# Attention transposes taken from TensorE to VectorE and DMA, in two sets of query blocks

## The chip, the cores and the metric

The kernel runs on one core of one Trainium2 chip. The metric is the device time of one execution in microseconds (us), the median of several runs. The kernel before takes 1697.11 us (three runs, 1695.94 to 1697.37).

## The reference, cut to what matters

The program is two transformer blocks one after the other over 512 tokens of width 1024. The change touches only the attention of the first block. It has 8 heads of width 64. Keys lie in two blocks of 256; each query sees all earlier keys (with two blocks, the selection of past blocks takes the one there is), so what is computed is plain causal attention with a distance bias:

```
s = q @ k^T * 64**-0.5 - slope[head] * (query - key), masked where key > query
p = softmax(s)
out[query] = sum over keys of p[query, key] * v[key]
y_attn = out @ w_branch_attn
```

The last product contracts over keys. TensorE contracts over partitions, so for it both v and p must lie with the key on the partition. The projection leaves v with the head's columns on the partitions, and the softmax runs with the query on the partitions. Both must be turned.

## The kernel before

**Matrix products in three parts.** Every float32 product is made of three: weights are split into a rounded part w_hi (ScalarE, L1259, 128x2048) and the rest w_lo (GpSimd, L454, four pieces of 128x512), the operand into a_hi and a_lo. A tile of 128 output columns by 512 tokens takes 24 matmuls of 128x512: 16 against w_hi (L504 and L505) and 8 against w_lo (L511). Weights come in panels of 1 MB, two tiles each, into two buffers w_raw, loaded by SyncE (L418) as soon as w_lo of the panel two before is made.

**A pair of heads.** `pair_of_heads` on TensorE runs four times, the first in straight code, the other three as a loop. One pair has four panels and eight tiles: q, k, v, a pool input, and four gate tiles. In order: tiles 0 to 3, between whose thirds stand the score products of the four query blocks (`scores`, L655); `turn_v`, four transposes of 128x128 (L661) of v_s into the PSUM bank aux 2; tile 4 (in the first pair it stands ahead of `turn_v`); tiles 5, 6 and 7, behind whose nine thirds `turn_probs` (L672) is spread, eight calls with 4, 4, 3, 3, 2, 2, 1 and 1 transposes; then `values` (L681), eight matmuls of probs_t with v_n. So TensorE makes 24 transposes in each pair, 96 in all.

**The other engines in a pair.** VectorE (L1855 to L1874) takes each score block from PSUM, adds the distance bias, finds the row's maximum, and one step later divides the exponentials (ScalarE, L1305) by their sum; then it stores tiles 4 to 7. Block qt of a head lies in `probs[head][:, qt, :]` and has 128 (qt + 1) keys. ScalarE copies each turned bank into v_n (L1319) and probs_t (L1312), with the rounding of the weights of panel 4i+4 between the fourth and the fifth of these, and that of 4i+5 after the last. Then it copies the pair's result (L1326), and VectorE makes its low part (L1881).

**What sets the order.** Each engine runs its instructions in written order and waits on semaphores. SyncE's queue before holds nothing in this stage but the loads of the weights. An instruction that waits holds up all behind it on its engine.

## Time and profile before

| | |
|---|---|
| median of three runs | 1697.11 us |
| span of the profiled execution, first to last instruction | 1694.9 us |
| TensorE busy | 1684.5 us (99%) |
| VectorE, ScalarE, GpSimd busy | 874.7, 706.1, 793.1 us (52%, 42%, 47%) |
| DMA moved | 193.84 MB, mean 114 GB/s |
| granted TensorE clock, mean | 0.997 |
| the four pairs of heads | 0 to 221 us |

The page's last matmul ends some microseconds before the span does, and of what a run's time holds around the span the profile shows nothing; the median lies 2.2 us above the span. To read the table: TensorE is busy nearly without a gap. How busy the other engines are says little by itself; what counts is when their results come.

### The profile page before, as it was taken

The numbers are of one execution on the slowest core, as the hardware profiler recorded it, in microseconds if no ns is written. First come the engines' busy times: TensorE is split into PE (matmuls) and PEld (weight loads), VectorE is DVE, ScalarE is ACT, GpSimd is POOL, SyncE is SP. The second block draws the span as 40 slices with busy tenths as digits, with TensorE's granted clock in tenths as the row PEclk, the third lists the DMA queues.
The fourth block names the chain that finished last, engine by engine and source line by source line (L and its number), as shares of the span: only waits on it lengthen the run. The fifth ranks groups of instructions, "written<-read, shape, count | busy, mean of one in ns | idle before, by whom it ended". The sixth has DMA issues, their size and how long they took to land.

```text
span 1694.9 us, 21874 instructions
## 1 busy us (share of the span) xinstructions
PE 1684.5 (99%) x7963; PEld 1374.6 (81%) x7963; DVE 874.7 (52%) x1365; ACT 706.1 (42%) x977; POOL 793.1 (47%) x605
## 2 busy tenths in 40 slices
PE   9999999999999999999999999999999999999998
PEld 7777778788888888888878888788888888888887
DVE  6234374563616167797897878863355511101113
ACT  5333364431313134456464554784424422222232
POOL 2434354444545455543434344444545544654453
PEclk9999999999999999999999999999999999999999
DMA  5222222274636342233222332222222222332232
GB/s 187 99 75 74 74 104 82 81 261 157 229 117 225 122 151 100 93 106 125 100 100 101 117 104 99 99 75 99 76 99 100 76 98 99 129 127 91 99 124 100
DMA packets 32540, 193.84 MB, mean 114 GB/s; under 512 B 3648, under 2 KB 5696, under 8 KB 13792
## 3 DMA queue, kind: packets, MB, share of 16 engines
q1 hardware_dynamic: 25376, 158.89, 26.5%
q10 hardware_dynamic: 7104, 34.15, 5.8%
q8 instruction: 38, 0.62, 0.1%
q14 instruction: 22, 0.18, 0.0%
HBM read 190.86 MB, written 2.16 MB: 114 GB/s over the span
## 4 chain that ended last, share of the span: by engine, by line
PE 98%; DMA 0%; DVE 0%; ACT 0%; SPq 0%; issue 0%; DVEq 0%
PE gemm_bank L511 25%; PE gemm_bank L504 25%; PE gemm_bank L505 25%; PE gemm_bank L542 4%; PE gemm_bank L558 4%; PE gemm_bank L551 3%; PE gemm_bank L546 1%; PE gemm_bank L789 1%; PE aux_bank L975 1%; PE aux_bank L655 1%; PE aux_bank L980 1%; PE aux_bank L960 1%; PE aux_bank L681 1%; PE aux_bank L672 1%; DMA w_raw<-weights_dram 0%; PE aux_bank L953 0%
## 5 line engine op out<-in xcount | busy, mean ns | idle before, releaser
L454 POOL TENSOR_TENSOR w_lo<-w_raw,w_hi 128x512 fp32r<-128x512 f32 x580 | 771.5, 1362 | 881.6 <-ACT w_hi L1259 870.4
L504 PE MATMUL gemm_bank<-a_hi,w_hi 128*128 128x512 f32 x1008 | 402.6, 399 | 0.0
L505 PE MATMUL gemm_bank<-a_lo,w_hi 128*128 128x512 f32 x1008 | 393.2, 390 | 0.0
L1259 ACT ACTIVATE w_hi<-w_raw 128x2048 fp32r<-128x2048 f32 x145 | 276.5, 1907 | 187.1 <-PE gemm_bank L511 122.7
L504 PE MATMUL gemm_bank<-b_hi,w_hi 128*128 128x512 f32 x688 | 267.8, 389 | 0.0
L505 PE MATMUL gemm_bank<-b_lo,w_hi 128*128 128x512 f32 x688 | 267.7, 389 | 0.0
L511 PE MATMUL gemm_bank<-a_hi,w_lo 128*128 128x512 f32 x1024 | 258.7, 395 | 0.0
L511 PEld LDWEIGHTS gemm_bank<-a_hi,w_lo 128*128 128x128 f32 x1024 | 190.2, 188 | 45.0 <-issue 6.2
L504 PEld LDWEIGHTS gemm_bank<-a_hi,w_hi 128*128 128x128 f32 x1008 | 189.3, 188 | 43.9 <-issue 5.6
L505 PEld LDWEIGHTS gemm_bank<-a_lo,w_hi 128*128 128x128 f32 x1008 | 189.4, 188 | 39.4 <-issue 1.9
L2161 DVE SCALAR_TENSOR_TENSOR aux_bank<-scratch,gcol,aux_bank 128x511 f32<-128x511 f32 (+15 forms) x240 | 165.8, 734 | 14.2 <-ACT aux_bank L1485 11.9
L511 PE MATMUL gemm_bank<-b_hi,w_lo 128*128 128x512 f32 x688 | 170.6, 389 | 0.0
L511 PEld LDWEIGHTS gemm_bank<-b_hi,w_lo 128*128 128x128 f32 x688 | 129.1, 188 | 26.8
L505 PEld LDWEIGHTS gemm_bank<-b_lo,w_hi 128*128 128x128 f32 x688 | 129.2, 188 | 26.8
L504 PEld LDWEIGHTS gemm_bank<-b_hi,w_hi 128*128 128x128 f32 x688 | 129.1, 188 | 26.7
L2461 DVE TENSOR_TENSOR arena<-arena,gemm_bank 128x512 f32<-128x512 f32 x21 | 14.4, 688 | 174.6 <-PE gemm_bank L511 173.1
L2394 DVE SCALAR_TENSOR_TENSOR h<-gemm_bank,mod,h 128x512 f32<-128x512 f32 x23 | 17.3, 751 | 108.6 <-PE gemm_bank L511 104.9
L504 PE MATMUL gemm_bank<-f_hi,w_hi 128*128 128x512 f32 x165 | 64.2, 389 | 0.0
L505 PE MATMUL gemm_bank<-f_lo,w_hi 128*128 128x512 f32 x165 | 64.2, 389 | 0.0
L1735 ACT ACTIVATE f_hi<-arena 128x512 f32 (+1 forms) x22 | 13.9, 632 | 115.9 <-DVE arena L2461 115.0
L2202 DVE SCALAR_TENSOR_TENSOR sq<-gemm_bank,gcol,sq 128x511 f32<-128x511 f32 (+2 forms) x72 | 53.8, 748 | 13.2 <-ACT sq L1505 11.5
L1393 ACT ACTIVATE b_hi<-gemm_bank 128x512 fp32r<-128x512 f32 x31 | 18.6, 599 | 100.5 <-DVE gemm_bank L2006 100.5
(414 smaller groups left out, 2133.4 us busy)
## 6 DMA issues: line engine op xcount, KB each, us to landing
w_raw<-weights_dram SPq DMA_DIRECT2D x146, 1024.0 KB, 4.7
arena<-ada_dram ACTq DMA_DIRECT2D x32, 768.0 KB, 4.7
acc<-cum_rows ACTq DMA_DIRECT2D x8, 512.0 KB, 3.7
h<-x_t_dram SPq DMA_DIRECT2D x8, 256.0 KB, 5.9
row_b<-cum_rows ACTq DMA_DIRECT2D x4, 512.0 KB, 4.8
scratch<-cum_rows ACTq DMA_DIRECT2D x4, 512.0 KB, 4.2
out_t_dram<-a_raw SPq DMA_DIRECT2D x7, 256.0 KB, 2.2
w_raw<-weights_dram SPq DMA_DIRECT2D x4, 256.0 KB, 5.2
```

Source lines behind the costliest of these rows:

```text
L454: ins = pool.tensor_tensor(wlo[s][:, w], raw[s][:, w], whi[s][:, w].bitcast(F32), ALU.subtract)
L504: pe.matmul(gemm_bank[bank][:, :], whi[slot][:, w], hi[:, k, :], start=(n == 0), stop=False)
L505: pe.matmul(gemm_bank[bank][:, :], whi[slot][:, w], lo[:, k, :], start=False, stop=False)
L511: mm = pe.matmul(gemm_bank[bank][:, :], wlo[slot][:, blk * P:blk * P + P], hi[:, k, :], start=False, stop=(n == last))
L542: pe.matmul(gemm_bank[t % 4][:, :], whi[panel % 2][:, w], hi[:, k, :], start=(n == 0), stop=False)
L551: pe.matmul(gemm_bank[t % 4][:, :], wlo[panel % 2][:, blk * P:blk * P + P], hi[:, k, :], start=False, stop=False)
L558: mm = pe.matmul(gemm_bank[t % 4][:, :], whi[panel % 2][:, blk * P:blk * P + P], lo[:, k, :], start=False, stop=(n == last))
L1259: act.activation(whi[panel % 2][:, :], raw[panel % 2][:, :], ACT.Copy).then_inc(w_hi_ready, 1)
L1393: act.activation(b_hi[:, j, :], bank, ACT.Square).then_inc(b_hi_ready, 1)
L2161: dve.scalar_tensor_tensor(aux[q][:, d:S], u_buf[:, q, 0:S - d], gc(G_CONV_W + CONV_TAPS * q + CONV_TAPS - 1 - d), aux[q][:, d:S], ALU.mul ...
L2202: ins = dve.scalar_tensor_tensor(acc[:, d:S], bank[:, 0:S - d], gc(G_SSM_W + SSM_TAPS * n + SSM_TAPS - 1 - d), acc[:, d:S], ALU.mult, ALU.add)
L2394: dve.scalar_tensor_tensor(hk, gemm_bank[t % 4][:, :], g_, hk, ALU.mult, ALU.add).then_inc(h_ready, 1)
```

## The change

v and the probabilities are no longer turned by TensorE.

- VectorE turns 32x32 blocks (`dve.transpose`): v_s into turned_v once v is stored and the pool tile is stored, and each query block of each head into `turned_p` as soon as it is divided by its sum. Within a partition it writes the blocks in another order, so that a transfer has rows of 128 elements.
- SyncE stores these to DRAM (`store_turned`, 256 KB each in pieces of 512 B: two for each query block, one for v) and loads them back with the 32-partition groups exchanged (four transfers for v, and in `move_turned` eight transfers of 128 KB for each half of the query blocks, each into 32 partitions). A load waits until the stores it needs have landed.
- ScalarE copies from the loaded squares into v_n and probs_t (`in_place`), query blocks 0 and 1 first, then the rounding of panel 4i+4, then blocks 2 and 3.
- TensorE's tiles 5 to 7 run without anything between; `values` waits for ScalarE's nine copies (values_ready).
- The loads of the weights now stand in SyncE's queue among these transfers: panels 4i+3 and 4i+4 ahead of them, 4i+5 and 4i+6 behind them.
- GpSimd clears the first three blocks of both turned_p at the start. Three semaphores are merged with others or dropped.

```
-                def turn_v():
-                    pe.wait_ge(bank_free[2], 2 * i + 2)
-                    for t in range(QT):
-                        mm = pe.transpose(aux[2][:, t * P:(t + 1) * P], v_s[:, t * P:(t + 1) * P], ident[:, :])
-                    mm.then_inc(t_done, 1)
-
-                def turn_probs(n):
...
-                    for qt in range(j, QT):
-                        mm = pe.transpose(bank[:, qt * P:(qt + 1) * P], probs[head][:, qt, j * P:(j + 1) * P], ident[:, :])
...
                 def values():
-                    pe.wait_ge(t_read, 9 * i + 9)
+                    pe.wait_ge(values_ready, 9 * i + 9)
...
+            def store_turned(i, qt, count):
+                sp.wait_ge(turned, 9 * i + count)
+                for head in range(2):
+                    sp.dma_start(probs_dram[head][:, :, qt, :], turned_p[head][:, qt, :].rearrange("k (g x) -> k g x", g=QT)) \
+                        .then_inc(turned_stored, 16)
+            def move_turned(first, end):
+                for head in range(2):
+                    to = turned_p[head][:, first:end, :].rearrange("k t n -> k (t n)").rearrange("k (p x) -> k p x", p=QT)
+                    rows = probs_dram[head].rearrange("(p k) g t x -> k p g t x", p=QT)[:, :, :, first:end, :] \
+                        .rearrange("k p g t x -> k p g (t x)")
+                    for g in range(QT):
+                        sp.dma_start(to[32 * g:32 * g + 32], rows[:, :, g, :]).then_inc(probs_moved, 16)
+            load(2, 0)
+            with sp.Fori(0, PAIRS) as i:
+                load(4 * i + 3, 1)
+                load(4 * i + 4, 0)
+                store_turned(i, 0, 2)
+                store_turned(i, 1, 4)
+                sp.wait_ge(turned, 9 * i + 5)
+                sp.dma_start(v_dram, turned_v.rearrange("k (g x) -> k g x", g=QT)).then_inc(turned_stored, 16)
+                sp.wait_ge(turned_stored, 16 * 9 * i + 16 * 5)
+                rows = v_dram.rearrange("(p k) g x -> k p g x", p=QT)
+                for g in range(QT):
+                    sp.dma_start(v_raw[32 * g:32 * g + 32, :].rearrange("k (p x) -> k p x", p=QT), rows[:, :, g, :]) \
+                        .then_inc(v_moved, 16)
+                move_turned(0, 2)
+                store_turned(i, 2, 7)
+                store_turned(i, 3, 9)
+                sp.wait_ge(turned_stored, 16 * 9 * i + 16 * 9)
+                move_turned(2, 4)
+                load(4 * i + 5, 1)
+                load(4 * i + 6, 0)
...
+                def in_place(half):
+                    act.wait_ge(probs_moved, 256 * i + 128 * half + 128)
...
+                        for t in range(2):
+                            qt = 2 * half + t
+                            act.activation(probs_t[head][:, 0:qt + 1, qt * P:(qt + 1) * P].rearrange("k j (p e) -> k j p e", p=QT),
+                                           moved[:, t, 0:qt + 1, :, :], ACT.Copy).then_inc(values_ready, 1)
...
+                        dve.wait_ge(bank_free[2], 2 * i + 2)
+                        dve.transpose(turned_v.rearrange("q (g c e) -> q c g e", g=QT, c=QT),
+                                      v_s.rearrange("q (c g e) -> q c g e", c=QT, g=QT)).then_inc(turned, 1)
...
+                            dve.wait_ge(probs_ready, 8 * i + u + 1)
+                            dve.transpose(turned_p[head][:, qt - 1, :].rearrange("k (g j e) -> k j g e", g=QT, j=QT)[:, 0:qt, :, :],
+                                          probs[head][:, qt - 1, 0:n].rearrange("q (j g e) -> q j g e", j=qt, g=QT)) \
+                                .then_inc(turned, 1)
```

On TensorE, at the end of the first pair of heads, the rows before are these (gemm_bank3 is tile 7, aux_bank0 and aux_bank2 take the turned probabilities, L681 is `values`):

```order
L505 MATMUL gemm_bank3<-a_lo_49,w_hi1 128x512
L504 MATMUL gemm_bank3<-a_hi,w_hi1 128x512
L505 MATMUL gemm_bank3<-a_lo_49,w_hi1 128x512
L672 MATMUL aux_bank0<-ident,arena 128x128 [waits t_read]
L672 MATMUL aux_bank2<-ident,scratch 128x128 [waits t_read]
L511 MATMUL gemm_bank3<-a_hi,w_lo1 128x512 x8
L681 MATMUL aux_bank3<-arena 64x512 [waits b_lo_ready,t_read]
L681 MATMUL aux_bank3<-scratch,arena 64x512
```

and in the changed kernel, at the same place:

```order
L550 MATMUL gemm_bank3<-a_lo_49,w_hi1 128x512
L549 MATMUL gemm_bank3<-a_hi,w_hi1 128x512
L550 MATMUL gemm_bank3<-a_lo_49,w_hi1 128x512
L556 MATMUL gemm_bank3<-a_hi,w_lo1 128x512 x8
L709 MATMUL aux_bank3<-arena,row_b 64x512 [waits b_lo_ready,values_ready]
L709 MATMUL aux_bank3<-scratch,row_b 64x512
```

The transposes between the thirds of a tile are gone, and the first matmul of `values` waits for ScalarE's copies instead of the last turned bank.

On SyncE, the whole loop that loads weights before:

```order
L415 ISA
L418 ISA [waits w_lo_ready]
L418 DMA w_raw0<-weights_dram 128x2048
L418 ISA [waits w_lo_ready]
L418 DMA w_raw1<-weights_dram 128x2048
L415 REGISTER_ALU
L415 COMPARE_AND_BRANCH
```

and in the changed kernel the part of the loop over pairs from the first half of the moves on (probs_turned_rows is the DRAM copy, arena and scratch hold the two heads' turned_p):

```order
L437 DMA arena<-probs_turned_rows0 32x4x256 x4
L437 DMA scratch<-probs_turned_rows1 32x4x256 x4
L426 REGISTER_ALU
L428 DMA probs_turned_rows0<-arena 512x1x128 [waits turned]
L428 DMA probs_turned_rows1<-scratch 512x1x128
L426 REGISTER_ALU
L428 DMA probs_turned_rows0<-arena 512x1x128 [waits turned]
L428 DMA probs_turned_rows1<-scratch 512x1x128
L455 REGISTER_ALU
L437 DMA arena<-probs_turned_rows0 32x4x256 [waits turned_stored]
L437 DMA arena<-probs_turned_rows0 32x4x256 x3
L437 DMA scratch<-probs_turned_rows1 32x4x256 x4
```

The stores of query blocks 2 and 3 stand behind the moves of the first half, and the moves of the second half behind a wait for all stores.

On ScalarE, from the copy of v on, before:

```order
L1319 ACTIVATE arena<-aux_bank2 128x512 [waits t_done]
L1310 REGISTER_ALU
L1312 ACTIVATE arena<-aux_bank0 128x512 [waits t_done]
L1310 REGISTER_ALU
L1312 ACTIVATE scratch<-aux_bank2 128x512 [waits t_done]
L1310 REGISTER_ALU
L1312 ACTIVATE arena<-aux_bank0 128x384 [waits t_done]
L1310 REGISTER_ALU
L1312 ACTIVATE scratch<-aux_bank2 128x384 [waits t_done]
L1256 REGISTER_ALU
L1259 ACTIVATE w_hi0<-w_raw0 128x2048 [waits tile_done,w_loaded0]
```

and in the changed kernel, from the copies of the first half on:

```order
L1336 ACTIVATE arena<-arena 128x128 [waits probs_moved]
L1336 ACTIVATE arena<-arena 128x2x128
L1336 ACTIVATE scratch<-scratch 128x128
L1336 ACTIVATE scratch<-scratch 128x2x128
L1277 REGISTER_ALU
L1280 ACTIVATE w_hi0<-w_raw0 128x2048 [waits tile_done,w_loaded0]
L1330 REGISTER_ALU
L1336 ACTIVATE arena<-arena 128x3x128 [waits probs_moved]
L1336 ACTIVATE arena<-arena 128x4x128
L1336 ACTIVATE scratch<-scratch 128x3x128
L1336 ACTIVATE scratch<-scratch 128x4x128
L1280 ACTIVATE w_hi1<-w_raw1 128x2048 [waits tile_done,w_loaded1]
```

The eight copies from PSUM have become eight copies within SBUF; the last four come with one wait for the second half of the moves.

## Rows read from the trace of the kernel before

**Rows 1.** The page: TensorE's busy time, and the chain that ended last

```profile
PE 1684.5 (99%) x7963; PEld 1374.6 (81%) x7963; DVE 874.7 (52%) x1365; ACT 706.1 (42%) x977; POOL 793.1 (47%) x605
...
PE 98%; DMA 0%; DVE 0%; ACT 0%; SPq 0%; issue 0%; DVEq 0%
```

**Rows 2.** TensorE's waits up to 225 us: line, what it waited for, us, times, longest

```profile
PE aux_bank L577 <- POOL ident L434: 1.4, 1, 1.4
```

**Rows 3.** Timeline of TensorE, first two pairs of heads: start us, us, line, tiles

```profile
38.78 2.12 PE L511 MATMUL gemm_bank<-a_hi,w_lo 128*128 128x512 f32 x8
...
60.03 0.64 PE L681 MATMUL aux_bank<-arena 128*64 128x512 f32 x1
...
73.34 0.39 PE L504 MATMUL gemm_bank<-a_hi,w_hi 128*128 128x512 f32 x1
...
76.97 1.98 PE L511 MATMUL gemm_bank<-a_hi,w_lo 128*128 128x512 f32 x8
...
87.95 0.66 PE L661 MATMUL aux_bank<-ident,arena 128*128 128x128 f32 x4
...
112.79 0.64 PE L681 MATMUL aux_bank<-arena 128*64 128x512 f32 x1
```

**Rows 4.** Timeline of VectorE in the second pair of heads

```profile
83.19 0.41 DVE L1861 TENSOR_REDUCE neg_max<-scratch 128x1 f32<-128x256 f32 x1
...
88.06 0.75 DVE L1855 SCALAR_TENSOR_TENSOR arena<-dist,slopes,aux_bank 128x512 f32<-128x512 f32 x1 [0.31 <-PE aux_bank L655]
...
90.57 0.68 DVE L1842 TENSOR_TENSOR arena<-gemm_bank,acc 128x512 f32 x1
...
92.48 1.44 DVE L1874 TENSOR_SCALAR scratch<-scratch,row_inv 128x384 f32<-128x384 f32 x1
...
95.27 0.47 DVE L1874 TENSOR_SCALAR scratch<-scratch,row_inv 128x512 f32<-128x512 f32 x1
```

**Rows 5.** Timeline of GpSimd and of ScalarE in the second pair of heads

```profile
89.79 5.28 POOL L454 TENSOR_TENSOR w_lo<-w_raw,w_hi 128x512 fp32r<-128x512 f32 x4 [9.22 <-ACT w_hi L1259]
...
96.36 0.60 ACT L1312 ACTIVATE arena<-aux_bank 128x512 f32<-128x512 f32 x1 [4.26 <-PE aux_bank L672]
...
103.39 1.91 ACT L1259 ACTIVATE w_hi<-w_raw 128x2048 fp32r<-128x2048 f32 x1
...
115.31 0.60 ACT L1326 ACTIVATE b_hi<-aux_bank 128x512 f32 x1 [0.44 <-PE aux_bank L681]
```

**Rows 6.** The page's DMA issues: KB each, median us from issue to landing

```profile
w_raw<-weights_dram SPq DMA_DIRECT2D x146, 1024.0 KB, 4.7
...
h<-x_t_dram SPq DMA_DIRECT2D x8, 256.0 KB, 5.9
...
out_t_dram<-a_raw SPq DMA_DIRECT2D x7, 256.0 KB, 2.2
```

**Rows 7.** SyncE's issues of lines 410 and 418: ns min/median/max of one issue

```profile
L410 SPq DMA_DIRECT2D h<-x_t_dram x8: 424/433/711, 1.7 to 6.8; - x8
...
L418 SPq DMA_DIRECT2D w_raw<-weights_dram x144: 332/333/343, 15.6 to 1654.3; - x144
```

**Rows 8.** DMA of the last 10 us in 40 slices, all transfers of 1 KB pieces

```profile
GB/s 0 0 0 25 331 352 290 356 343 348 75 83 360 343 281 344 348 327 33 0 0 0 0 99 356 339 286 352 348 294 352 339 352 348 331 348 95 0 0 0
```

**Rows 9.** Stretches: us, busy time (instructions) by engine, granted clock, DMA share, GB/s

```profile
672.00:674.00 2.00, 2.00 (x11) 2.00 (x11) 1.02 (x6) 0.29 (x3) 2.00 (x3) 0.50 0.01 4
678.00:680.00 2.00, 2.00 (x10) 1.64 (x9) 1.90 (x3) 0.73 (x1) 2.00 (x3) 0.98 0.89 377
1690.00:1692.00 2.00, 0.00 (x0) 0.00 (x0) 2.00 (x6) 0.00 (x0) 0.00 (x0) 0.96 0.57 189
1692.00:1694.90 2.90, 0.00 (x0) 0.00 (x0) 0.28 (x1) 0.00 (x0) 0.00 (x0) 0.50 0.70 231
```

**Rows 10.** Timeline of TensorE ahead of the two stretches with a lower clock

```profile
668.65 0.95 PE L842 MATMUL aux_bank<-ones,dist 128*128 128x1 f32 x8
...
1688.30 0.71 PE L1221 MATMUL aux_bank<-ident,rinv 128*128 128x128 f32 x4 [0.17 <-DVE rinv L2497]
```

More of the change, by code:

```diff
@@ L166, in build @@
         sq_acc = acc31[:, 0, :]
+        turned_v, v_raw = tmp[:, 0, :], tmp[:, 1, :]
         first_sq = arena[:, 0:8, :]
@@ L413, in _, with load @@
             sp.dma_start(poolw[:, :, :], poolw_in).then_inc(poolw_loaded, 16)
-            with sp.Fori(1, P_END // 2) as i:
-                for s in range(2):
-                    sp.wait_ge(w_lo_ready, 2 * i + s - 1)
-                    sp.dma_start(raw[s][:, :], w_in[bass.ds(2 * i + s, 1)].rearrange("a p n -> (a p) n")) \
-                        .then_inc(w_loaded[s], 16)
+            def load(m, slot):
+                sp.wait_ge(w_lo_ready, m - 1)
+                sp.dma_start(raw[slot][:, :], w_in[bass.ds(m, 1)].rearrange("a p n -> (a p) n")) \
+                    .then_inc(w_loaded[slot], 16)
@@ L420, in _ @@
+            load(4 * PAIRS + 3, 1)
+            with sp.Fori(2 * PAIRS + 2, P_END // 2) as i:
+                load(2 * i, 0)
+                load(2 * i + 1, 1)
             if P_END % 2:
@@ L431, in _ @@
         def _(pool):
-            pool.memset(ones[:, :], 1.0).then_inc(const_step, 1)
-            pool.wait_ge(const_step, 1)
+            pool.memset(ones[:, :], 1.0).then_inc(consts, 1)
+            pool.wait_ge(consts, 1)
             pool.affine_select(out=ident[:, :], in_=ones[:, :], compare_op=ALU.is_equal, fill=0.0, base=0,
@@ L446, in _ @@
                                pattern=[[1, P]], channel_multiplier=-1).then_inc(consts, 1)
+            for of in turned_p:
+                pool.memset(of[:, 0:3, :], 0.0).then_inc(consts, 1)
             def low_parts(i, s, pieces=range(LOW_PIECES), rounded=None):
@@ L709, in pair_of_heads @@
                         scores(part + 1)
-                    turn_v()
                     g(4)
-                turned_behind = ((), (), (0, 1), (2,), (3,), (4,), (5,), (6, 7), ()) if first else \
-                    ((0,), (1,), (2,), (3,), (4,), (5,), (6,), (7,), ())
-                for n in range(9):
-                    third(5 + n // 3, n % 3)
-                    for m in turned_behind[n]:
-                        turn_probs(m)
+                g(5), g(6), g(7)
                 values()
@@ L1306, in exps @@
                                        accum_out=row_sum[:, u:u + 1]).then_inc(exp_ready, 1)
-                def turned(n):
-                    head, j = n % 2, n // 2
-                    act.wait_ge(t_done, 9 * i + 2 + n)
-                    bank = aux[0 if n % 2 == 0 else 2]
-                    act.activation(probs_t[head][:, j, j * P:S], bank[:, j * P:S], ACT.Copy).then_inc(t_read, 1)
+                def in_place(half):
+                    act.wait_ge(probs_moved, 256 * i + 128 * half + 128)
+                    for head in range(2):
+                        moved = turned_p[head][:, 2 * half:2 * half + 2, :].rearrange("k t n -> k (t n)") \
+                            .rearrange("k (p t j e) -> k t j p e", p=QT, t=2, j=QT)
+                        for t in range(2):
+                            qt = 2 * half + t
+                            act.activation(probs_t[head][:, 0:qt + 1, qt * P:(qt + 1) * P].rearrange("k j (p e) -> k j p e", p=QT),
+                                           moved[:, t, 0:qt + 1, :, :], ACT.Copy).then_inc(values_ready, 1)
                 round_weights(i, P_PAIR + 2, 4, 2, 8)
@@ L1317, in _ @@
                 exps(3)
-                act.wait_ge(t_done, 9 * i + 1)
-                act.activation(v_n, aux[2][:, :], ACT.Copy).then_inc(t_read, 1)
-                for n in range(GH):
-                    turned(n)
-                    if n == 3:
-                        round_weights(i, P_PAIR + 4, 4, 6, 8)
+                act.wait_ge(v_moved, 16 * QT * i + 16 * QT)
+                act.activation(v_n.rearrange("k (c p e) -> k c p e", c=QT, p=QT),
+                               v_raw.rearrange("k (p c e) -> k c p e", p=QT, c=QT), ACT.Copy).then_inc(values_ready, 1)
+                in_place(0)
+                round_weights(i, P_PAIR + 4, 4, 6, 8)
+                in_place(1)
                 round_weights(i, P_PAIR + 5, 4, 8, 8)
```

54 lines of the change are left out of this document (26 added, 28 removed).

## The prediction

> **What bounds the kernel now.** I read the page first, then TensorE's waits, then the timelines of one pair of heads engine by engine, and last the DMA issues and the granted clock. TensorE is busy for 1684.5 us of a span of 1694.9, and it is 98% of the chain that ended last [rows 1]. In the attention stage (0 to 221 us) its longest wait is 1.4 us, and that is at the very start [rows 2]. Neither VectorE nor ScalarE nor a transfer is late for it. So each microsecond taken from TensorE here is a microsecond of the whole, as long as the replacement arrives before `values`, which is the one place in a pair that needs the turned data. The question is thus not how much is moved off TensorE but when the last copy lands in probs_t, against when TensorE now gets there.
>
> **What is removed.** A matmul of 128x512 follows another after 0.227 us: the 16 of a tile's high part start at 73.34 and the low part at 76.97, 3.63 us [rows 3]. A tile of 24 is 5.44 us, its low part 1.81. In the second pair TensorE is at the first transpose of v at 87.95 and at `values` at 112.79 [rows 3]; the four tiles between are 4 x 5.44 = 21.8 us, so without transposes it is there at 109.7. That takes away 3.1 us. In the first pair the low part of tile 4 starts at 38.78, and `values` at 60.03 [rows 3]: 38.78 + 1.81 + 3 x 5.44 = 56.9, again 3.1 us. Four pairs give 12.4 us, 24 transposes at 0.13 us each. This is all there is to gain, and it is solid.
>
> **What is added, on VectorE.** A transpose is an operation that the trace doesn't have. The nearest rows are the 128x512 divide in SBUF, 0.47 us, and the 128x512 operation at one element per cycle, 0.68; the 128x256 reduction is 0.41 [rows 4]. I take one element per cycle (0.68, 0.55, 0.41, 0.28 for 512 to 128 keys), since an exchange between partitions is nearer to the plain form than to the doubled one; at half that speed the second half would be 2.5 us later, below zero it can't go. Two transposes of 128x256 stand before the last score block, where VectorE idles 0.31 us [rows 4]: it falls 0.5 us behind. The pool tile's store (90.57, 0.68) then ends at 91.75, and v is turned at 92.4. The divide of 92.48 took 1.44 us beside GpSimd's low parts (89.79 to 95.07) against 0.47 for the larger one of 95.27 [rows 4, 5]: a transpose of v that is held the same way would be up to 1.3 us later. I take none. The last divide ended at 95.75; with 0.5, with v's 0.7 and with the four last transposes (2.5) the last block is turned at 99.4. VectorE has no other work until tile 5 is stored, and nothing of that is urgent, so the time itself is free.
>
> **What is added, on SyncE and in the transfers.** SyncE does these one after the other. A store of 256 KB in 1 KB pieces lands 2.2 us after its issue [rows 6]. Here the pieces are 512 B; I take 2.4, between 2.2 and the 4.7 of a transfer four times as large. An issue costs 0.43 us with a fixed address [rows 7]. So in the second pair:
> - v is turned at 92.4 and its store has landed at 94.8;
> - four moves of v and eight of the first half, 12 x 0.43 = 5.2, to 100.0. VectorE's 99.4 is hidden behind it;
> - four stores of blocks 2 and 3: the last is issued at 101.3 and has landed at 103.7;
> - eight moves: the last is issued at 106.7, lands 2.2 later, 108.9;
> - ScalarE's four copies: 0.60 for 512 keys [rows 5], and by proportion 0.50 for 384, twice, 2.2 us, to 111.1.
>
> TensorE is there at 109.7 and waits 1.4 us. The first pair has the same chain 49.2 us earlier (87.95 against 38.78), since its tile 4 stands ahead of the last scores: the chain ends at 61.9, TensorE is there at 56.9, and waits 5.0. That is the least with these prices: 5.0 + 3 x 1.4 = 9.2 us of waits against 12.4 gained.
>
> **The price of the moves.** Eight moves carry 1.05 MB. The output's 1 KB pieces ran at about 350 GB/s [rows 8], which makes 3.0 us, less than the 3.4 of issuing. But those spanned all 128 partitions, and each of the moves goes into 32; no row has such a load. At half of the 350 they are 6.0 us, 2.5 more than the issuing, and both halves pay: the stores of blocks 2 and 3 queue behind the first half on the same DMA engines. That is 5 us more in each pair. A transfer behind others is slow here: the 256 KB pieces of x landed after 5.9 us each [rows 6]. I take the middle, 2.5 us more per pair: waits of 7.5 in the first pair and 3.9 in each other, 19.2 us.
>
> [...]
>
> **The clock.** After its last matmul (1688.30 + 0.71 = 1689.0) the granted clock was still 0.96 on average in 1690 to 1692 and 0.50 after, so it fell at 1691.8, 2.8 us into the idle stretch [rows 9, 10]. It also was 0.50 in 672 to 674, after a stretch of 128x1 products from 668.65, and was back (0.98) only in 678 to 680 [rows 9, 10]. [...] Six microseconds at half cost three. I take 2 for the first pair and 2 for the other three together (3.9 us is only just over 2.8), bounds 0 and 3 for each pair.
>
> **What stays hidden.** ScalarE rounds panel 4i+4 after the first half's copies. These can start when the last move of the first half lands (issued at 99.6, 2.2 later, 101.8) and are smaller than the 2.2 us of the second half, so the rounding (1.91, at 103.39 before [rows 5]) comes at the same time. The load of panel 4i+5 is issued after the moves, at 107, and lands at about 112 to 114 (4.7 alone [rows 6]); its panel is needed two tiles, 11 us, after `values`. ScalarE's copy of the result (115.31 before [rows 5]) stands behind that rounding, so it comes up to 1.5 us later after `values`. Only the last pair feels it, whose b_hi and b_lo the branch tiles need at once: 0.7 us. GpSimd's clearing of turned_p stands at the very start, where its queue has nothing else for this stage: nothing.
>
> **Sum.** -12.4 + 19.2 + 4 + 0.7 = +11.5. The span 1694.9 becomes 1706.4, and the median, 2.2 above the span, 1708.6. I put it at 1708.
>
> **Rivals.**
> - Transfers limited by issuing alone. For it: 350 GB/s with 1 KB pieces. Waits 9.2, the clock falls in the first pair only (2), 0.7: -0.5, 1696.6 us. This is no change.
> - The data is in time, the kernel is faster. SyncE's issues with a register address took 0.33, not 0.43 (the 144 loads of line 418 [rows 7]). If the new ones do too, 22 issues in the chain save 2.2 us, and 2.2 instead of 2.4 for each of the two stores 0.4. The three later pairs then never wait, the first waits 2.4: -12.4 + 2.4 = -10, 1687 us. It wins from the point where the four waits together are under 12.4 us. Against it: the chain of four trips (out and back for v, out and back for the second half) has 17.3 us from v's turning to `values` in three pairs (92.4 to 109.7), but 13.7 in the first (43.2 to 56.9), so there a wait stays in any case.
> - Half rate into 32 partitions. Waits of 10.0 and 3 x 6.4 = 29.2, the clock falls in each pair (8): -12.4 + 29.2 + 8 + 0.7 = +25.5, 1722.6 us. For it: no row shows so narrow a load reach 350. [...]
> - The change doesn't do what it says: the transposes stay or are elsewhere on TensorE. The order shows them gone; I give it nothing.
>
> **How the numbers follow.** The forecast (waits outlast the gain by a few us, with the clock) has 0.42, its own range 1700 to 1717. The half rate has 0.17, issuing alone 0.18, in time 0.23. A measurement tells 0.2%, 3.4 us, from no change. Faster are the last case and a little of issuing alone, 0.26; same is most of issuing alone, 0.15; slower the rest, 0.59. The range leaves out about half of the in-time case and half of the half-rate case: 1689 to 1722.
>
> **What would show it.** Right: TensorE's waits list a new row at `values` in each pair, on ScalarE's copies, with the first about 3.6 us longer than the other three, and a granted clock of 0.5 behind it; the moves' landing well over 2.2 us; transposes of 128x512 near 0.68 us. Wrong: no wait at `values` after the first pair (then 1687), or VectorE's last transpose later than 100 us in the second pair. If transposes of 128x512 take 1.3 us, VectorE and not SyncE sets the chain, and all comes 2 us later.

## The result

The changed kernel takes 1716.65 us (median of four runs, 1716.29 to 1718.36), the kernel before 1696.97 beside it on the same chip (1695.94 to 1697.37). The ratio is 1.0122, 95% interval 1.0109 to 1.0134: slower by 1.2%. The forecast was 1708, with a range of 1689 to 1722 and a chance of 0.59 for slower. The direction is right and the time lies inside the range, but the size is short: +19.7 us in the median (and in the span, 1714.6 against 1694.9) where the sum gave +11.5.

### The profile page after: what moved, and what is told of

Same layout as the page of the kernel before. It is cut to its first block, busy times and chain, and to the rows that moved or that the text cites. A ratio compares the mean times of both kernels' runs of the same rounds, so it can differ in the third digit from the quotient of the medians.

```text
span 1714.6 us, 21798 instructions
## 1 busy us (share of the span) xinstructions
PE 1680.9 (98%) x7867; PEld 1367.7 (80%) x7867; DVE 882.6 (51%) x1401; ACT 705.6 (41%) x977; POOL 795.3 (46%) x607
## 4 chain that ended last, share of the span: by engine, by line
PE 91%; SPq 3%; DMA 3%; DVE 2%; issue 1%; ACT 1%; DVEq 0%
PE gemm_bank L549 23%; PE gemm_bank L556 23%; PE gemm_bank L550 23%; PE gemm_bank L587 4%; PE gemm_bank L603 4%; PE gemm_bank L596 3%; SPq L437 1%; PE gemm_bank L591 1%; PE gemm_bank L810 1%; PE aux_bank L709 1%; PE aux_bank L996 1%; DMA probs_turned_rows<-scratch 1%; DMA scratch<-probs_turned_rows 1%; PE aux_bank L1001 1%; PE aux_bank L981 1%
## 5 line engine op out<-in xcount | busy, mean ns | idle before, releaser
L2495 DVE TENSOR_TENSOR arena<-arena,gemm_bank 128x512 f32<-128x512 f32 x21 | 14.4, 688 | 174.6 <-PE gemm_bank L556 173.1
L2428 DVE SCALAR_TENSOR_TENSOR h<-gemm_bank,mod,h 128x512 f32<-128x512 f32 x23 | 17.3, 751 | 108.6 <-PE gemm_bank L556 104.9
L2236 DVE SCALAR_TENSOR_TENSOR sq<-gemm_bank,gcol,sq 128x511 f32<-128x511 f32 (+2 forms) x72 | 53.8, 748 | 13.2 <-ACT sq L1530 11.5
```

What stands on the lines that cost most here:

```text
L2236: ins = dve.scalar_tensor_tensor(acc[:, d:S], bank[:, 0:S - d], gc(G_SSM_W + SSM_TAPS * n + SSM_TAPS - 1 - d), acc[:, d:S], ALU.mult, ALU.add)
L2428: dve.scalar_tensor_tensor(hk, gemm_bank[t % 4][:, :], g_, hk, ALU.mult, ALU.add).then_inc(h_ready, 1)
```

## The profile after

The page of the changed kernel, TensorE's busy time, the chain that ended last, and four DMA issues (KB each, median us from issue to landing):

```profile
PE 1680.9 (98%) x7867; PEld 1367.7 (80%) x7867; DVE 882.6 (51%) x1401; ACT 705.6 (41%) x977; POOL 795.3 (46%) x607
...
PE 91%; SPq 3%; DMA 3%; DVE 2%; issue 1%; ACT 1%; DVEq 0%
...
probs_turned_rows<-arena SPq DMA_DIRECT2D x16, 256.0 KB, 3.0
probs_turned_rows<-scratch SPq DMA_DIRECT2D x16, 256.0 KB, 3.2
arena<-probs_turned_rows SPq DMA_DIRECT2D x32, 128.0 KB, 2.9
scratch<-probs_turned_rows SPq DMA_DIRECT2D x32, 128.0 KB, 3.3
```

Against [rows 1] TensorE has 96 instructions less, and its share of the chain falls from 98% to 91%. What takes its place is SyncE's queue, the transfers and VectorE. The waits of TensorE in the attention stage (0 to 240 us; total, times, longest), in which [rows 2] had nothing but the 1.4 at the start:

```profile
PE aux_bank L709 <- ACT scratch L1336: 22.9, 4, 9.2
```

L709 is `values`, L1336 ScalarE's copy of the second set of query blocks. The timeline of TensorE has the four waits in brackets; the rows of L587 are the first product of the next pair (or of the branch tiles):

```profile
66.83 1.11 PE L709 MATMUL aux_bank<-arena,row_b 128*64 128x512 f32 x1 [9.24 <-ACT scratch L1336]
...
70.57 0.73 PE L587 MATMUL gemm_bank<-a_hi,w_hi 128*128 128x512 f32 x2
...
122.92 1.11 PE L709 MATMUL aux_bank<-arena,row_b 128*64 128x512 f32 x1 [4.65 <-ACT scratch L1336]
...
127.39 0.92 PE L587 MATMUL gemm_bank<-a_hi,w_hi 128*128 128x512 f32 x2
...
179.49 1.11 PE L709 MATMUL aux_bank<-arena,row_b 128*64 128x512 f32 x1 [4.21 <-ACT scratch L1336]
...
183.23 0.96 PE L587 MATMUL gemm_bank<-a_hi,w_hi 128*128 128x512 f32 x3
...
235.77 1.11 PE L709 MATMUL aux_bank<-arena,row_b 128*64 128x512 f32 x1 [4.84 <-ACT scratch L1336]
...
240.24 2.18 PE L587 MATMUL gemm_bank<-b_hi,w_hi 128*128 128x512 f32 x8
```

A product of 128x512 at L709 shows 1.11 us where it was 0.64 [rows 3]: it runs at half the clock. From `values` to the next tile it takes 3.74, 4.47, 3.74 and 4.47 us; before it took 2.30 each time (in the last pair 218.33 to 220.63). Together that is 7.2 us. The granted clock of the second pair (the sixth number behind the length, those in brackets not counted; columns as in [rows 9]):

```profile
118.00:120.00 2.00, 0.27 (x2) 0.00 (x0) 0.69 (x1) 0.00 (x0) 1.04 (x1) 1.00 1.06 233
120.00:122.00 2.00, 0.00 (x0) 0.00 (x0) 0.00 (x0) 1.18 (x3) 0.00 (x0) 0.74 1.00 384
122.00:126.00 4.00, 3.08 (x10) 1.07 (x12) 0.00 (x0) 2.69 (x3) 0.00 (x0) 0.50 0.74 291
126.00:128.00 2.00, 2.00 (x12) 1.26 (x9) 0.00 (x0) 0.41 (x2) 1.91 (x2) 0.55 0.00 0
```

TensorE went idle at 118.27, the granted clock halved (from 1.00 to 0.50) at 121.0 (1.00 for half of 120 to 122, 0.50 for the rest, gives 0.74), and it was back at about 127.8, just behind the products of `values` (0.55 in 126 to 128).

**VectorE did as foreseen.** Its timeline in the second pair, v's transpose (L1891) and the last block's (L1907):

```profile
99.66 0.70 DVE L1891 STREAM_TRANSPOSE tmp<-arena 128x512 f32<-128x512 f32 x1
...
100.77 1.45 DVE L1902 TENSOR_SCALAR scratch<-scratch,row_inv 128x384 f32<-128x384 f32 x1
...
102.15 0.56 DVE L1907 STREAM_TRANSPOSE arena<-arena 128x384 f32<-128x384 f32 x1
...
104.67 0.67 DVE L1907 STREAM_TRANSPOSE scratch<-scratch 128x512 f32<-128x512 f32 x1
```

0.70 for 128x512 and 0.56 for 128x384 stand beside 0.68 and 0.55 in the forecast, and the divide beside GpSimd is as slow as in [rows 4] (1.45 us and 1.44). What the forecast calls one element per cycle is 1.04 ns an element here (L1886, a row maximum over 128 keys 0.28 us and over 512 0.68), and its doubled form 0.52 ns (L1902, 0.28 and 0.48); how long a cycle is no trace tells. The last transpose ends at 105.34, well before SyncE asks for it (the store of this block is issued at 109.40). Counted from the start of the pair, 8.24 us later than before the change, that is 97.1 against 99.4 in the forecast; hidden either way.

**The chain of transfers.** SyncE's timeline in the same pair, one row for issues in a row (start, time of all of them):

```profile
100.39 0.34 SPq L446 DMA_DIRECT2D v_turned_rows<-tmp  x1
102.41 1.76 SPq L450 DMA_DIRECT2D tmp<-v_turned_rows  x4
104.22 1.85 SPq L437 DMA_DIRECT2D arena<-probs_turned_rows  x4
106.11 1.85 SPq L437 DMA_DIRECT2D scratch<-probs_turned_rows  x4
108.08 0.52 SPq L428 DMA_DIRECT2D probs_turned_rows<-arena  x1
108.64 0.65 SPq L428 DMA_DIRECT2D probs_turned_rows<-scratch  x1
109.40 0.66 SPq L428 DMA_DIRECT2D probs_turned_rows<-arena  x1
110.10 0.75 SPq L428 DMA_DIRECT2D probs_turned_rows<-scratch  x1
113.91 1.73 SPq L437 DMA_DIRECT2D arena<-probs_turned_rows  x4
115.69 1.85 SPq L437 DMA_DIRECT2D scratch<-probs_turned_rows  x4
```

and the chain of waits in this stretch, its DMA pieces (start us, us):

```profile
110.10 3.80 DMA probs_turned_rows<-scratch
...
117.11 3.69 DMA scratch<-probs_turned_rows
```

An issue of a move takes 0.43 us, as foreseen, and with a gap of 0.04 one comes every 0.47. The four stores take 2.8 us to issue and not 1.7, the last lands 3.8 us after its issue and not 2.4, the last move 3.7 after its own and not 2.2. In the DMA's slices from 108 to 121 us (0.33 us each) the stores run at up to 348 GB/s, the rate of [rows 8]; then there is an idle stretch of over 1 us between the last bytes and the moves; the moves run at 210 to 310:

```profile
GB/s 271 262 218 211 255 262 227 321 340 348 340 333 329 317 320 285 104 0 0 0 0 79 208 277 255 252 306 246 246 255 221 214 221 243 388 177 176 416 410 403
```

## The experiments

Ratios are to the kernel before, run beside each; its median there was 1696.0 to 1697.0 us, so a difference between two of the changed kernels that were run at different times is good to about 1 us. Waits and timelines are those of the one profiled run of each. "+x.x" is us after the store of v is issued, in the second pair unless said otherwise. In the changed kernel: stores of blocks 2 and 3 issued +7.7 to +10.5, landed +13.5, second moves issued by +17.2, landed +20.4, TensorE there at +17.9.

**no_trips: is the loss all in the trips?** The transfers to DRAM and back are gone; ScalarE copies from VectorE's output.

```
-    act.wait_ge(probs_moved, 256 * i + 128 * half + 128)
+    act.wait_ge(turned, 9 * i + 4 + 5 * half)
-    (SyncE: store_turned, move_turned and both transfers of v)
```

> The changed kernel without its trips through DRAM: VectorE turns the 32x32 blocks as before, ScalarE makes the same nine copies straight from VectorE's buffers, SyncE loads only weights. The groups of 32 partitions are not exchanged, so the attention is of wrongly placed numbers. Theory A (the whole loss is the wait for the transfers and the clock behind it): TensorE waits nowhere at `values`, the clock stays at 1.00 in the attention stage, and the 12.4 us of transposes are saved in full: 1697.0 - 12.4 = 1684.6 us, 0.9927 of before. Rival (VectorE's turning or ScalarE's copies are themselves late): a wait of over 1 us at `values` stays, and the time is above 1688 us.

Measured: 1684.99 us, ratio 0.9933 (0.9916 to 0.9949), no wait at `values`, granted clock 0.999. Taking the transposes off TensorE is worth 11.5 us (12.4 in the forecast), and VectorE's and ScalarE's parts of the new path cost nothing. All of the loss lies in the transfers, between VectorE's transposes and ScalarE's copies.

**clock_kept: what is the clock's part?** TensorE fills most of the wait with products that nobody reads.

```
+    pe.wait_ge(s_read, 8 * i + 8)
+    for _ in range(36 if first else 18):
+        pe.matmul(aux[1][:, :], a_hi[:, 0, 0:P], a_hi[:, 1, :], start=True, stop=True)
     pe.wait_ge(values_ready, 9 * i + 9)
```

> The changed kernel with products of 128x512 that nobody reads, on TensorE in front of the wait at `values`: 36 in the first pair (8.2 us), 18 in each other (4.1 us), less than the waits measured there (9.2, 4.7, 4.2, 4.8 us). If a part of the loss is the clock that falls in the wait, the products behind it run at full speed: the stretch from the start of `values` to the next pair's first product is 2.3 us again instead of 3.7 to 4.5, and the time falls by 6 to 9 us, to about 1709. If the clock costs nothing beyond the wait, the time stays at 1716.7.

Measured: 1710.92 us, ratio 1.0085 (1.0068 to 1.0102), 5.7 less than the changed kernel. Its TensorE timeline in the second pair:

```profile
117.06 4.24 PE L706 MATMUL aux_bank<-a_hi 128*128 128x512 f32 x18
122.69 0.64 PE L712 MATMUL aux_bank<-arena,row_b 128*64 128x512 f32 x1 [1.39 <-ACT scratch L1339]
...
125.00 3.92 PE L587 MATMUL gemm_bank<-a_hi,w_hi 128*128 128x512 f32 x16
```

`values` still comes 5.5 us after the last tile (its low part ends at 117.2), but its products take 0.64 us again and the next tile starts 2.31 later, as before the change, in all four pairs: 7.2 us less. From the last tile to `values` it is 9.7, 5.5, 4.6 and 5.0 us here, 1.8 more in all than the 22.9 of the changed kernel (in the second pair one move of the first half is issued 1.5 us late; the rest is open). The two leave 5.4, and the spans of the two profiles are 5.3 apart (1714.6 and 1709.3). So 7.2 us is what the clock costs, and the 5.7 of the medians is that less the longer waits.

**wide_moves: do 32 partitions make the moves slow?** The same sixteen moves of 128 KB a pair, each into all 128 partitions; the exchange of the groups is left out.

```
-    sp.dma_start(to[32 * g:32 * g + 32], rows[:, :, g, :]).then_inc(probs_moved, 16)
+    sp.dma_start(to[:, g, :], rows[:, g, :]).then_inc(probs_moved, 16)
```

> The changed kernel with each of the moves into 128 partitions of 1 KB instead of 32 partitions of 4 KB: the same number of transfers, bytes and pieces of 1 KB, the groups of 32 partitions not exchanged. Theory A (a load into 32 partitions is slow, some 235 GB/s while the DMA engines are busy): the eight moves run near 345 GB/s, the stores behind the first half start 1 us sooner and the second half lands 1 us sooner; the waits at `values` fall by about 2 us each, 8 us in all, and with a clock that falls less the time is 1705 to 1709. Theory B (SyncE's issuing, 0.46 us each, sets the pace whatever the width): the waits fall by under 0.5 us each, 1715 to 1717.

Measured: 1716.26 us, ratio 1.0117 (1.0100 to 1.0134): nothing gained. The page's DMA issues, and the DMA pieces of its chain in the second pair:

```profile
arena<-probs_turned_rows SPq DMA_DIRECT2D x32, 128.0 KB, 2.5
scratch<-probs_turned_rows SPq DMA_DIRECT2D x32, 128.0 KB, 2.7
```

```profile
109.18 5.66 DMA probs_turned_rows<-scratch
118.07 2.88 DMA scratch<-probs_turned_rows
```

By the page's medians a wide move lands 0.4 to 0.6 us sooner than a narrow one, and the last of this pair 0.8 sooner (2.88 against 3.69), but they are issued at the same pace of 0.47 us, and in this pair the stores ahead landed after 5.7 us in place of 3.8, for which no run gives a cause. Over the four pairs the waits are 22.4 us against 22.9. The narrow moves of the changed kernel ran at 210 to 310 GB/s together. Why the width counts for so little no run shows.

**two_queues and two_queues_late: is it the issuing?** ScalarE's queue issues four of the second half's eight moves. In the first, SyncE's next load of weights is thereby issued beside them; in the second it waits until the moves have landed.

```
-    move_turned(2, 4)
+    move_turned(2, 4, (0,))          # head 1: four act.dma_start behind round_weights
+    sp.wait_ge(probs_moved, 256 * i + 256)      # two_queues_late alone
```

> The changed kernel with the second head's four moves of the second half issued by ScalarE, at the same time as SyncE issues the first head's. All else is the same and the result complete. Theory A (the DMA engines are the limit, busy 0.9 and more while the moves run into 32 partitions): the last move lands at most 0.7 us sooner, 1713 to 1717. Theory B (the issuing is the limit): four issues of 0.46 us less in the chain, 1.8 us less wait in each pair, 1706 to 1710.

> As two_queues (ScalarE issues four of the last eight moves), but SyncE holds the load of the weights of panel 4i+5 until all moves have landed. Theory: two_queues was slower (1723.9) because the 1 MB load was issued 1.8 us sooner and was served in turns with ScalarE's moves, which landed after 4.6 us. Then this kernel has waits below the changed kernel's (22.9 us in all) by 1 to 1.5 us each, and lies at 1710 to 1714, if the later weights hold nothing up. If it is ScalarE's issuing that is slow, it stays above 1720.

Measured: 1723.94 us, 1.0164 (1.0147 to 1.0181), and 1719.59 us, 1.0135 (1.0120 to 1.0151). Neither beats the change. Neither time lies where a theory had it. In two_queues_late the eight issues took 1.8 us in place of 3.6, and the last piece of its chain is

```profile
117.22 5.84 DMA scratch<-probs_turned_rows
```

against 3.69 above: what issuing gives back, the transfer takes. The last move lands 7.2 us after the first issue of the half, where it was 6.9, and the waits are 24.7 us. In two_queues, where the megabyte of weights ran beside the moves, they are 28.9. Whether ScalarE's queue is slower by itself was not separated from this. Lifting the width alone or the issuing alone gains nothing.

**wide_few: both limits at once.** One move of 512 KB over 128 partitions for each head and half, in place of four; the exchange is left out.

```
-    for g in range(QT):
-        sp.dma_start(to[32 * g:32 * g + 32], rows[:, :, g, :]).then_inc(probs_moved, 16)
+    sp.dma_start(to, rows).then_inc(probs_moved, 16)
```

> The changed kernel with one move of 512 KB for each head and half, into 128 partitions, instead of four of 128 KB: the same bytes in the same 1 KB pieces, 4 issues in a pair instead of 16; the groups of 32 partitions are not exchanged. Sixteen wide moves gave nothing (1716.3), so if SyncE's issuing (0.46 us each) paces the moves, this one gains: the second half lands about 1.3 us sooner (1.05 MB at 345 GB/s is 3.0 us against 3.7 of issuing), and the stores behind the first half start sooner by about 1: waits shorter by 1.5 to 2.5 us in each pair, 1705 to 1710. If the DMA engines or the landing are the limit and the issuing is not, the time stays within 2 us of 1716.

Measured: 1711.79 us, ratio 1.0085 (1.0070 to 1.0101): 4.9 us less than the change, only part of it. Its four runs lie far apart (1708.70 to 1715.78), and the profiled one is the slowest, with a span of 1714.1 us and waits of 20.9; so this trace shows the least of the gain. Its chain in the second pair:

```profile
108.42 6.57 DMA probs_turned_rows<-scratch
115.61 4.88 DMA scratch<-probs_turned_rows
```

The last store is issued at +7.3 in place of +9.7 and lands at +13.8 in place of +13.5. The likely reason is the megabyte of the first half's moves, which the DMA engines still had to carry; this run alone doesn't show it.

**long_stores: the pieces of 512 B.** The stores write 2 KB pieces, the moves read otherwise ordered rows (the result is in another order).

```
-    sp.dma_start(probs_dram[head][:, :, qt, :], turned_p[head][:, qt, :].rearrange("k (g x) -> k g x", g=QT))
+    sp.dma_start(probs_dram[head][:, qt, :, :].rearrange("k t x -> k (t x)"), turned_p[head][:, qt, :])
```

> The changed kernel with the stores of the probabilities as 128 pieces of 2 KB each instead of 512 of 512 B, and the moves from that layout (still eight of 128 KB for each half, 1 KB pieces; the blocks come back in another order). If the 512 B pieces make the store dear, a store's issue goes from 0.52 and 0.64 us to 0.34 (as v's does) and its landing from 3.0 to 2.2: four stores in the chain take 1.4 us of issuing instead of 2.8, the waits fall by 1 to 1.5 us in each pair, and the time is 1709 to 1712. If the landing is made of something fixed, 1715 to 1717.

Measured: 1721.24 us, ratio 1.0151 (1.0135 to 1.0166): slower than the change, waits 28.4. An issue of a store fell from 0.52 and 0.65 to 0.36 and 0.43 us, yet the last store of the second pair landed 4.6 us after its issue and the last move 6.1. The theory failed; a cheap issue by itself brought nothing. Why the moves out of that layout take longer stays open.

**stores_first2: the order of the queue.** The stores of blocks 2 and 3 stand ahead of the first half's moves, and each half counts on a semaphore of its own.

```
-    move_turned(0, 2)
     store_turned(i, 2, 7)
     store_turned(i, 3, 9)
+    move_turned(0, 2)
```

> SyncE issues the four stores of blocks 2 and 3 before the eight moves of blocks 0 and 1 instead of behind them; every transfer and every byte stays. Theory A (the second round trip starts too late, because eight issues stand ahead of its stores): in the changed kernel the second pair's stores went out 7.7 to 10.5 us behind the store of v and the second moves 13.5 to 17.2. Now the stores go out at 3.8 to 6.6, the first moves take the time in which the stores land, and the second moves go at 10.3 to 14.0: up to 3.2 us sooner. ScalarE's copies of the first set start about 2 us later, so that some 2 us are left: waits of TensorE 23 - 8 = 15 us, clock 1 us less, 1708. Theory B (the DMA engines' work in flight sets the end, whatever the order): the moves that now stand together are served at 210 to 260 GB/s, the last one lands as late as before, 1716. Theory C: ScalarE's later first set delays its weight rounding, slower than 1718.

Measured: 1713.87 us, ratio 1.0106 (1.0091 to 1.0122), 2.8 us less than the change. The waits are 19.6, 3.3 less, where the order theory wanted 8. The stores went out at +3.9 to +6.5, as asked. But the sixteen moves that now stand together are issued more slowly and land later (page: 4.0 and 4.3 us in place of 2.9 and 3.3); SyncE's timeline from the first half's moves on:

```profile
106.09 2.61 SPq L437 DMA_DIRECT2D arena<-probs_turned_rows  x4
108.74 1.85 SPq L437 DMA_DIRECT2D scratch<-probs_turned_rows  x4
110.71 1.79 SPq L437 DMA_DIRECT2D arena<-probs_turned_rows  x4
112.54 2.78 SPq L437 DMA_DIRECT2D scratch<-probs_turned_rows  x4
```

**few_first: both edits that helped.** stores_first2's order and wide_few's four moves a pair.

> Both edits at once that helped alone: one move of 512 KB over all 128 partitions for each head and half instead of four into 32 (1711.8 alone), and the stores of blocks 2 and 3 ahead of the first half's moves (1713.9 alone). The moves leave out the exchange of the partition groups; bytes in all stay. Counted from the store of v (stores go out at 3.9 to 6.5 us in the run with the stores first): the first moves are issued by 7.9, the stores have landed at 9.4, the second moves are issued by 10.8. Theory A (what is left is order and issuing): the last move lands 4 us after its issue, at 15, the copies end at 17.5, and TensorE is there at 17.9: waits in the first pair alone, some 4 us, clock 2: -12.4 + 6 + 1 = -5, 1691.6, ratio 0.997. Theory B (the DMA engines carry 3.1 MB from 3.9 on at the 240 GB/s seen in the second moves, 13 us, to 17; copies to 19): waits 1.2 in three pairs and 5.7 in the first, 9.3, clock 2: -12.4 + 9.3 + 2 + 1 = 0, 1696.5. Theory C (the two gains were the same one): 1711.

Measured: 1696.99 us, ratio 1.0004 (0.9994 to 1.0013). That is Theory B's number: the two edits give 4.9 and 2.8 us alone and 19.7 together (4.1, 1.8 and 18.9 if each is counted from the kernel before that ran beside it). Its TensorE waits, and its chain and SyncE's issues in the second pair:

```profile
PE aux_bank L707 <- ACT scratch L1334: 8.5, 4, 5.4
```

```profile
102.58 3.73 DMA probs_turned_rows<-scratch
...
106.89 7.11 DMA scratch<-probs_turned_rows
```

```profile
103.30 0.87 SPq L435 DMA_DIRECT2D arena<-probs_turned_rows  x1
104.21 0.87 SPq L435 DMA_DIRECT2D scratch<-probs_turned_rows  x1
106.33 0.52 SPq L435 DMA_DIRECT2D arena<-probs_turned_rows  x1
106.89 0.63 SPq L435 DMA_DIRECT2D scratch<-probs_turned_rows  x1
```

Its DMA slices from 100 to 116 us (0.4 us each), and the second pair's `values`:

```profile
GB/s 99 164 142 110 154 287 294 268 305 274 303 280 287 179 155 189 338 353 374 358 369 379 323 340 364 361 356 366 387 402 382 458 379 397 451 328 82 20 20 20
```

```profile
116.12 0.64 PE L707 MATMUL aux_bank<-arena,row_b 128*64 128x512 f32 x1 [1.50 <-ACT scratch L1334]
```

The second half is issued by +10.8 in place of +17.2, and the DMA engines never run dry between the stores (landed at 106.3) and the second moves: they carry the first half there. The copy starts at +17.3. The waits are 5.43 us in the first pair and 1.50, 0.87 and 0.74 in the others, and at the last three lengths the clock stays at 1.00 (the windows from 116 to 118, 166 to 168 and 216 to 218 us). The waits fell by 14.4 us and the clock gave back most of the rest, 5.7: only the first pair's stretch behind `values` is still long, 3.84 us. The rate is not the 240 GB/s of Theory B: behind 106.4 us the engines move 320 to 460, for the next megabyte of weights, issued at 107.73, runs beside the moves. Even so the path through DRAM only pays for itself. Whether four moves that do exchange the groups would run as fast was not tried.

**hybrid, packed_hybrid, packed_before: how much to move.** v and blocks 0 and 1, which have time, go by transfers; blocks 2 and 3 stay on TensorE (14 transposes a pair). In packed_hybrid two key columns share a bank, so the product stream is broken 4 times a pair instead of 8. packed_before is the kernel before with 7 breaks instead of 9.

```
+    for j in (2 * jp, 2 * jp + 1):              # packed_hybrid; in hybrid one j for each call
+        for qt in range(max(j, 2), QT):
+            mm = pe.transpose(bank[:, at:at + P], probs[head][:, qt, j * P:(j + 1) * P], ident[:, :])
```

> A mix: v and query blocks 0 and 1 are turned by VectorE and transfers as in the changed kernel, query blocks 2 and 3 by TensorE (14 of 24 transposes in each pair, spread behind the thirds of tiles 5 to 7 as in the kernel before); no second trip, ScalarE's in-place copies stand last. By the trace of the changed kernel the first half's moves have landed 10.6 us after v's store is issued, which is 6 us before `values`; so TensorE should wait nowhere there, the clock stays at 1.00, and ten transposes less (0.13 us each) in four pairs give 5.2 us: 1696.5 - 5.2 = 1691.3 us, 0.9969 of before. Rival: a copy by ScalarE comes late for a bank that TensorE wants, and the gain is under 2 us.

> v and query blocks 0 and 1 turned by VectorE and transfers, blocks 2 and 3 by TensorE as in the hybrid run before it, but its 14 transposes a pair in 4 breaks of the product stream instead of 8, two columns of blocks in one bank. Theory A (a break of the stream costs some 0.15 us, a transpose in it some 0.075): 4 breaks a pair less are 0.6 us, and the short waits of TensorE for ScalarE's copies stay under 0.5 us, 2.4 us in all: 1692.4 beside the 1694.8 of the hybrid, ratio 0.998 to the kernel before. Theory B (each transpose costs 0.13, whatever its place): 1694.8 again, ratio 0.999. Theory C (two columns in one bank make TensorE wait for ScalarE, 0.3 us a copy longer): 1697 or more.

> The kernel before, all on TensorE and ScalarE: its 24 transposes a pair in 7 breaks of the product stream instead of 9; the single transpose of column 3 goes into the free quarter of column 2's bank. Theory A (a break costs 0.15 us): 2 x 0.15 x 4 = 1.2 us less, ratio 0.9993. Theory B (a transpose costs the same anywhere): no change, ratio 1.0000. Both lie near what 5 rounds can tell; it says whether packing alone does what moving half of the transposes away does.

Measured: hybrid 1694.84 us, ratio 0.9992 (0.9983 to 1.0001); packed_hybrid 1692.93 us, 0.9981 (0.9972 to 0.9990); packed_before 1696.23 us, 1.0000 (0.9991 to 1.0009). hybrid has no wait for a transfer, but 0.9 us of waits for ScalarE's copies of turned banks, all in the first pair, and gains only 1.3 us where 5.2 was expected. From one `values` to the next its later pairs take 51.9 us against 52.8 before: ten transposes less give 0.9 a pair, and not 1.3. packed_hybrid is another 1.9 us faster and beats the kernel before by 3.1 us. But of the 1.9 some 1.4 stand in the first pair, with those 0.9; the later pairs differ by 0.1 each. In the kernel before, two breaks less bring nothing that can be measured, where 1.2 us was expected (a later pair takes 52.7 to 52.8 us either way); so a fixed price of 0.15 us for a break is not borne out. Against no_trips, whose later pairs take 49.9 us, the 24 transposes of the kernel before cost 0.12 us each and the 14 of hybrid 0.14; why is open.

## Why the prediction was right in direction and short in size

| step | forecast | measured |
|---|---|---|
| transposes removed | -12.4 | -10.8 (-11.0 in the trace of no_trips, -11.5 in its median) |
| waits at `values` | 7.5 + 3 x 3.9 = 19.2 | 9.24, 4.65, 4.21, 4.84: 22.9 |
| the same, from where `values` could start | | 4 x 0.07 = 0.3 |
| clock | 4 | 7.2 (`values` to next tile, four pairs) |
| last pair's b_hi, b_lo | 0.7 | nothing beyond the clock's part |
| sum | 11.5 | 19.6 of 19.7 |

How the measured column is read: the first product behind the four pairs starts at 220.63 before and at 240.24 after, 19.6 us later, and the rows above divide that. From the start of a pair to the modelled end of its last tile TensorE takes 60.10, 50.53, 50.53 and 50.52 us before and 57.59, 47.70, 47.90 and 47.70 after: 10.8 less (in the third, 0.2 is the clock, still low at its start). A wait is counted from the modelled end of the last product; where nothing is waited for, `values` starts 0.07 us ahead of that end (112.79 against 112.86), four times. From the last product of `values` to L587 it is 0.36 us in the last pair and 0.36 in the second, where b_hi is not needed; both are the 0.20 of before at half the clock.

**Right: the bound, VectorE, the mechanism.** v was turned at 92.4 in the forecast; its store was issued at 100.39, and the pair began 8.24 us later than before (70.57 against 62.33), which makes 92.15. That store is of 2 KB pieces (128 of them in the trace), not of 512 B as the text on the change has it, and landed after 2.0 us where 2.4 was taken. The row at `values` appeared in each pair, on ScalarE's copies, with a clock of 0.50 behind it. TensorE was there 17.9 us after v's turning (17.3 foreseen).

**Short by 3.7 us: the waits.** The chain to the last move's landing takes 20.4 us in the second pair; with issuing alone the forecast gave 16.5, with the middle for the moves 19.0. The step that failed is the extra of 2.5 us ("I take the middle"), which was to cover all that comes on top of issuing; it is 3.9. By its parts: the last store is issued 0.8 later ("An issue costs 0.43 us" holds for a move, but for the gap of 0.04, and not for a store with 512 B pieces, 0.52 to 0.75) and lands 1.4 later (3.8 and not 2.4, behind the first half's moves); the last move is issued 0.2 later and lands 1.5 later (3.7 and not 2.2). From the last landing to `values` it is 2.1 us and not 2.2, and TensorE arrives 0.6 later than foreseen, which leaves 0.7 of a wait in the second pair; in the third and fourth it is 0.3 and 0.9. The first wait is 1.7 over, 9.24 against 7.5, and there one issue of v's moves is long: 2.96 us for the four (45.36) against 1.76 in the other pairs. Why is open; no load of weights was issued or landing then.

The reason given for the extra holds only in part. It was taken as the middle between no price and the half rate into 32 partitions, and wide_moves shows the width to be worth 0.5 us of waits in all. The half rate, and with it the 2.5 us of the sum, was the author's estimate: no run shows it, and the moves into 32 partitions ran at 210 to 310 GB/s together. What the trace does bear out is the other half of that passage, that a transfer behind others lands late (3.8 and 3.7 us). That the extra came out as near as 2.5 against 3.9 is in part luck.

**Over by 1.6 us: the transposes.** The gain was called solid, at 3.1 us a pair. TensorE's stretch got 2.8 shorter, 0.12 us a transpose and not 0.13.

**Short by 3.2 us: the clock.** The forecast gave 2 us to the first pair and 2 to the other three together, since a wait of 3.9 "is only just over 2.8". The clock fell in all four, to 0.50 as in [rows 9], and each fall cost 1.4 to 2.2 us. The delay of 2.8 us, read from one place, was taken as a constant; in the trace after it was 1.9, 2.7, 3.7 and 2.7 us.

**The rivals.** "Half rate into 32 partitions" at 1722.6 is nearer to 1716.65 (6.0 us off) than the forecast of 1708 (8.7), but wide_moves shows its mechanism not to be the cause: the width alone is worth nothing. So a right number would have come from a wrong reason there. "Issuing alone" falls with the landings of 3.8 and 3.7 us in the trace, and with two_queues_late. "In time" wanted 0.33 us for an issue with a register address; only the first issue behind a wait took that (0.34 at 102.41, 0.31 at 113.91), the others 0.43. What fits all the runs is that the two cost about the same here, 0.47 us of issue and 0.4 to 0.6 us of transfer (128 KB at 210 to 310 GB/s) a move, so that lifting either leaves the other; and that each round trip waits for the one before to run dry. That the loss is all in the trips is shown by no_trips. This division of it is argued: wide_few changed width and number of the moves at once, and few_first the order as well.

## What to carry to other kernels

A gain on the engine that bounds the kernel is counted against the landing of the last piece, and a path through DRAM costs the sum of its stages: the issues ahead in the queue, the landing behind whatever is in flight (3.8 and 3.7 us here), the pause until the first bytes come back (over 1 us); in all 20 us for a pair where 18 were to be had. Where a chain has several limits of about the same size, test them together, since each alone will look small (nothing for the width or a second queue, 4.9 and 2.8 us for fewer moves and for the order, 19.7 for these two together). And a wait on TensorE costs more than its length once the clock falls behind it (here 7.2 us on top of 22.9), so what matters first is to bring it under the length at which that happens (3.5 us was over it in stores_first2, 1.5 us under it in few_first); move only the part that has time to spare (packed_hybrid).

## What the runs showed of the hardware

- The clock fell 1.9, 2.7, 3.7 and 2.7 us after TensorE's last product in the four pairs of the changed kernel, and 5.1 us after it in the first pair of few_first (idle from 57.68, granted clock 0.90 in 62 to 63 us). A wait of 3.5 us was enough for it (the fourth pair of stores_first2, whose row is below: 1.11 us a product), a wait of 1.5 us in few_first was not (0.64). In the changed kernel it cost 1.4 to 2.2 us each time.

```profile
233.58 1.11 PE L709 MATMUL aux_bank<-arena,row_b 128*64 128x512 f32 x1 [3.48 <-ACT scratch L1336]
```

- An issue on SyncE costs by the transfer's shape: 0.34 us for v's store of 256 KB (2 KB rows), 0.43 for a move, 0.36 and 0.43 for a store of a block in 2 KB pieces, 0.52 and 0.65 for one in 512 B pieces, and 1.13 for the last store of the first pair.
- A transpose of 32x32 blocks on VectorE takes 0.70 us for 128x512 in float32 and 0.56 for 128x384, as long as the sum of a PSUM bank and an accumulator of 128x512 beside it (0.68).
